# Step sizes of the recurrent mixer: high and low weights in one stationary operand, two passes of products in place of three

## The reference

```python
proj = h @ w_in                                    # h: 256 x 1024
z, xbc, dt, hq, hf, hi, hg = split_cols(proj, ...) # dt: 256 x 8 (SSM_HEADS = 8)
...
dt = jax.nn.softplus(dt.astype(F32) + dt_bias.astype(F32))
a_head = -jnp.exp(a_log.astype(F32))
y = ssd_chunked(xs, dt, a_head, b_in, c_in)        # uses dt, and cumsum(dt * a_head)
```

## Time and profile before

| | |
|---|---|
| device time, three runs | 950.36, 950.37, 950.72 us, median 950.37 us |
| span of the profiled execution | 948.0 us |
| around the span | the median is 2.37 us more than the span; the profiled execution's own device time is not listed |
| PE busy | 934.2 us, 99% |
| DVE busy | 682.3 us, 72% |
| ACT busy | 517.9 us, 55% |
| POOL busy | 92.4 us, 10% |
| mean granted TensorE clock | 0.998 of full speed |

### The profile page before, as it was taken

One profiled execution on the slowest core, in us unless ns is written; L12 is line 12 of the kernel. 1 busy time (PEld: TensorE's weight loads), 2 busy tenths in 40 slices (PEclk: granted clock), 3 DMA queues, 4 the chain that ended last, 5 costly groups with the idle time before them and its releaser, 6 DMA issues.

```text
span 948.0 us, 12990 instructions
## 1 busy us (share of the span) xinstructions
PE 934.2 (99%) x5253; PEld 813.3 (86%) x5253; DVE 682.3 (72%) x880; ACT 517.9 (55%) x711; POOL 92.4 (10%) x111
## 2 busy tenths in 40 slices
PE   8999999999999999999999999999999999999997
PEld 7998888888888898888888888889998888888885
DVE  5899857666657977866776666558999767666663
ACT  5887545444446656965544434468685545334432
POOL 2550200000011100100000000000233010000000
PEclk9999999999999999999999999999999999999999
DMA  9933666565545455146656565556423457656531
GB/s 288 338 129 125 196 230 212 191 204 190 205 141 200 126 175 177 45 134 222 222 181 198 180 197 178 177 157 215 141 90 111 134 158 248 216 179 196 183 109 44
DMA packets 106955, 166.94 MB, mean 176 GB/s; under 512 B 2896, under 2 KB 82848, under 8 KB 106768
## 3 DMA queue, kind: packets, MB, share of 16 engines
q1 hardware_dynamic: 104688, 158.23, 51.1%
q0 software_dynamic: 2208, 7.89, 2.4%
HBM read 165.06 MB, written 1.05 MB: 175 GB/s over the span
## 4 chain that ended last, share of the span: by engine, by line
PE 86%; DVE 7%; ACT 3%; DMA 3%; issue 1%; POOL 0%; ACTq 0%; DVEq 0%; POOLq 0%
PE ps L400 83%; PE ps L408 3%; DMA raw<-in_w_in 2%; DVE wl L1956 2%; DVE SC L2080 1%; ACT wh L1337 1%; DVE fs L2090 1%; ACT SC L1671 1%; ACT junk L1325 0%; DMA h<-in_x 0%; ACT SC L1743 0%; DVE xhl L2017 0%; DVE wl L2118 0%; DVE wl L1970 0%; DVE hs L1999 0%
## 5 line engine op out<-in xcount | busy, mean ns | idle before, releaser
L1956 DVE TENSOR_TENSOR wl<-raw,wh 128x2048 fp32r<-128x2048 f32 (+2 forms) x141 | 318.0, 2259 | 142.3 <-ACT wh L1337 142.2
L1337 ACT ACTIVATE wh<-raw 128x2048 fp32r<-128x2048 f32 (+2 forms) x150 | 281.9, 1886 | 155.3 <-PE ps L400 137.3
L400 PE MATMUL ps<-xhl,wh 128*128 128x512 f32 (+1 forms) x1248 | 254.6, 350 | 0.3 <-ACT wh L1406 0.3
L400 PEld LDWEIGHTS ps<-xhl,wh 128*128 128x128 f32 x1248 | 199.2, 190 | 26.9 <-issue 0.7
L400 PE MATMUL ps<-wh,xhl 128*128 128x512 f32 (+3 forms) x800 | 190.3, 379 | 0.0
L400 PEld LDWEIGHTS ps<-wh,xhl 128*128 128x128 f32 x800 | 142.5, 188 | 24.8
L400 PEld LDWEIGHTS ps<-xhl,wl 128*128 128x128 f32 x1008 | 135.6, 191 | 7.5
L400 PE MATMUL ps<-xhl,wl 128*128 128x256 f32 x1008 | 140.6, 282 | 0.0
L400 PE MATMUL ps<-wl,xhl 128*128 128x512 f32 (+3 forms) x403 | 102.1, 375 | 0.2 <-DVE wl L1970 0.2
L400 PE MATMUL ps<-wh,fh 128*128 128x512 f32 x304 | 91.0, 392 | 0.3 <-DVE fl L2320 0.3
L400 PE MATMUL ps<-wh,fl 128*128 128x512 f32 x304 | 90.2, 390 | 0.0
(11 more groups left out here) (297 smaller groups left out, 833.9 us busy)
## 6 DMA issues: line engine op xcount, KB each, us to landing
raw<-in_ffn_gate SPq DMA_DIRECT2D x22, 1024.0 KB, 5.4
raw<-in_ffn_up SPq DMA_DIRECT2D x22, 1024.0 KB, 5.4
raw<-in_ffn_down SPq DMA_DIRECT2D x22, 1024.0 KB, 4.9
raw<-in_w_up SPq DMA_DIRECT2D x16, 1024.0 KB, 5.4
raw<-in_w_down SPq DMA_DIRECT2D x16, 1024.0 KB, 5.1
raw<-in_s_w_in SPq DMA_DIRECT2D x14, 1024.0 KB, 5.3
raw<-in_w_in SPq DMA_DIRECT2D x9, 1024.0 KB, 9.8
raw<-in_a_w_in SPq DMA_DIRECT2D x6, 1024.0 KB, 5.3
```

What stands on the lines that cost most here:

```text
L400: return e.matmul(o, a, b, start=start, stop=stop, skip_group_check=True)
L1337: e.activation(high_of(i), raw_of(i), ACT.Copy).then_inc(*up("act_high", i))
L1956: e.tensor_tensor(low_of(i), raw_of(i), high_of(i).bitcast(F32), ALU.subtract).then_inc(*up("dve_lo", i))
```

## The change

The high and low parts of the step weights stand side by side in one tile `wdt_hl` (columns 0 to 63 and 64 to 127). In the window of tile k the high columns still feed PSUM rows 0 to 7, and the low columns feed PSUM rows 64 to 71 of the same matmul. Two passes, with `xh` and with `xl`, give both groups of rows: 16 matmuls in place of 24. The product low x low, which was left out before, is now in the sum. The rows 64 to 71 are then added: ACT copies them from PSUM to `dr` row 1, and DVE adds rows 0 to 7, the bias and `dr` row 1 in one instruction. DVE makes the low part of the step weights earlier, right after `norm_low(5, 1)`. POOL zeroes 56 columns of one tile in place of 120 columns of two.

```diff
-        wdt_h, wdt_l = (sb(n, [128, 184], F32R) for n in ("wdt_h", "wdt_l"))
+        wdt_hl = sb("wdt_hl", [128, 184], F32R)
@@ tensor: recurrent()
-                for n, (w, x) in enumerate(((wdt_h, xh), (wdt_h, xl), (wdt_l, xh))):
-                    if n != 1:
-                        e.wait_ge(*(at("dve_dt_low") if n else at("act_dt_high")))
+                e.wait_ge(*at("dve_dt_low"))
+                for x in (xh, xl):
                     for k in range(8):
 
-                        d = mm(ps[0][:, 0:256], w[:, 8 * k:8 * k + 128], x[:, k, :], n == 0 and k == 0, n == 2 and k == 7)
+                        d = mm(ps[0][:, 0:256], wdt_hl[:, 8 * k:8 * k + 128], x[:, k, :], x is xh and k == 0, x is xl and k == 7)
                 d.then_inc(*up("pe_dt"))
@@ scalar: recurrent()
-                e.activation(wdt_h[:, 0:64], wdt, ACT.Copy).then_inc(*up("act_dt_high"))
+                e.activation(wdt_hl[:, 0:64], wdt, ACT.Copy).then_inc(*up("act_dt_high"))
@@
                 e.activation(st[R, 61:62], P("alog")[R], ACT.Exp).then_inc(*up("act_rate"))
+                e.wait_ge(*at("pe_dt"))
+                e.activation(dr[R, 1, :], ps[0][64:72, 0:256], ACT.Copy).then_inc(*up("act_dt_part"))
                 softplus("dt", *(dr[R, i, :] for i in range(4)), junk[R, 0:256])
@@ vector: recurrent()
                 norm_low(5, 1)
+                e.wait_ge(*at("act_dt_high"))
+                e.tensor_tensor(wdt_hl[:, 64:128], wdt, wdt_hl[:, 0:64].bitcast(F32), ALU.subtract).then_inc(*up("dve_dt_low"))
                 lows(S["hi"][0] + 4)
-                e.wait_ge(*at("act_dt_high"))
-                e.tensor_tensor(wdt_l[:, 0:64], wdt, wdt_h[:, 0:64].bitcast(F32), ALU.subtract).then_inc(*up("dve_dt_low"))
                 R = slice(0, 8)
-                e.wait_ge(*at("pe_dt"))
-                e.tensor_scalar(dr[R, 0, :], ps[0][R, 0:256], P("dtb")[R], None, ALU.add).then_inc(
+                e.wait_ge(*at("act_dt_part"))
+                e.scalar_tensor_tensor(dr[R, 0, :], ps[0][R, 0:256], P("dtb")[R], dr[R, 1, :], ALU.add, ALU.add).then_inc(
                     *up("dve_softplus", "dt", "x"))
                 lows(S["hi"][1] + 4)
@@ gpsimd
-            e.memset(wdt_h[:, 64:184].bitcast(F32), 0.0)
-            e.memset(wdt_l[:, 64:184].bitcast(F32), 0.0).then_inc(*up("pool_zero_dt_pad"))
+            e.memset(wdt_hl[:, 128:184].bitcast(F32), 0.0).then_inc(*up("pool_zero_dt_pad"))
```

More of the change, by code:

```diff
@@ L48 @@
                       "act_exp act_map_turned act_latent_out act_back"),
-    "act_recurrent": ("act_bound act_xs act_score act_seg_rows act_dt_high act_hq act_forget act_keys act_log_forget act_rate act_z act_hi act_decay act_between "
+    "act_recurrent": ("act_bound act_xs act_score act_seg_rows act_dt_high act_dt_part act_hq act_forget act_keys act_log_forget act_rate act_z act_hi act_decay act_between "
                       "act_xbc act_hg act_xb act_xs act_cb act_seg act_gated_square act_silu"),
```

## The result

| | median us | range | executions |
|---|---|---|---|
| before | 950.32 | 949.51 to 951.16 | 18 |
| changed | 951.63 | 950.48 to 952.58 | 18 |

The ratio is 1.0015, 95% interval 1.0009 to 1.0022: the change makes the kernel slower by 1.3 us, 0.9 to 2.1. The forecast was 951.5, within 0.2% of the time before.

The account below looks back on a forecast made before the run. PE, busy 99% of the span, was taken as the bound. Products -1.10, wait at xbc3 +1.98, rest of the wait at `score(8)` +0.28 give +1.16 us: span 949.2, time 951.5 us; 8 in 10 for 950.2 to 952.8.

Parts of the forecast that it names:

- PE's saving: At the step sizes: eight fewer matmuls and no wait for the low part start hf0 1.10 us earlier.
- The hand-over: After the step-size products: DVE waits for ACT's copy, then adds it; DVE 1.35 us late at mend, bounds 1.05 to 1.65.
- xbc3: PE's first meeting with late DVE: waits some 1.9 us for the turned step sizes, gain becomes a 0.88 us loss.
- `score(8)`: PE's second meeting: ACT, hanging on DVE, has 0.19 us in hand at queries(1); start 1.16 us late, lasting to the end.
- the likeliest case: Whole kernel: a loss of about 1.2 us, inside the 1.9 us a measurement can tell; chance 0.72.
- The 2.37 us between span and time: Whole kernel: median of runs lies 2.37 us above the profiled span; same distance added to the forecast span of 949.2.
- The clock rival: At the wait before xbc3: PE's clock falls to 1.2 GHz, adding 2.6 us, 954.1 us in all; chance 0.08.
- The absorption rival: DVE between 652 and 674 us: slack absorbs the delay, the 1.10 us saving stands, 949.3 us; between 949.3 and 950.9: 0.14.

Follow-up runs that it names:

- hand-over alone: Kernel before, still three passes and 24 matmuls, plus only ACT's copy of PSUM rows 64 to 71 and DVE's adding of it; 951.16 us, ratio 1.0011.
- turned first: Changed kernel with DVE's copies of the turned step sizes out of bank 0 moved ahead of conv(0); 951.10 us, ratio 1.0010.
- the longer wait: Changed kernel with DVE's copies of the turned step sizes moved behind the low part of hq0; 954.38 us, ratio 1.0047.
- both ends: Changed kernel with ACT's copy and alog exp earlier, xbc1's low part later, turned step sizes copied before conv(0), decays earlier; 948.54 us, ratio 0.9984.

## Why the prediction was right

**PE's saving**: forecast 1.10 us at hf0, found 1.12. The low part of the step weights is made at 630.2, long before.

**The hand-over**: the copy took 0.38 us (0.42 forecast), the sum 0.47 (0.47), Abs waited 0.54 behind the copy. The low part of xbc1 stood between the sum and `1+u`, as forecast, and Ln waited 0.24 us for `1+u`. `mend` came 1.42 us late, against 1.35. The load of xbc1 has a part in that: it lands when it does, and ACT starts the chain behind it. In the profiles ACT's table load at the head of the chain starts 3.49 us after the step sizes before, 3.64 and 3.63 in the two of the changed kernel, 3.41 in the hand-over alone and 3.47 in turned first. DVE was late by 1.42, 1.41, 1.19 and 1.26 there. Taken from that start the hand-over cost 1.26 to 1.28 us in all four, 0.08 under my sum, and the landing added up to 0.15.

**xbc3**: a PE wait of 1.9 us was forecast, 1.87 found (by the starts 1.98 forecast and 2.03 found, 30.90 to 32.93 us after the step sizes); PE 0.88 late there, 0.91 found.

**`score(8)`**: forecast 1.16 us late; 1.25 in the execution in which the clock stayed, and ACT's wait for PE was gone as forecast. From there to the end both kernels take 252.77 us, so the shift stays. This is the likeliest case as it was written, within 0.1 us at each step. That the median of runs (951.63) lies 0.13 from the forecast is partly luck: it stands between the two groups, 950.8 and 952.3. The forecast was for the group in which the clock stays up, and that one lost 0.85 and 0.62 us by its times, not 1.16; executions with the lower clock, which the forecast had left to a rival, brought the median up to it. The 2.37 us between span and time in the forecast did no harm, because adding them to both kernels is the same as adding 1.16 to the time before, but it is no constant: the executions of the changed kernel lie 1.8 us above their spans.

**The clock rival** was given 0.08 and 2.6 us on top. That the clock would leave 1.00 behind the wait was one of the signs that the prediction had named for being wrong, and in the profiled execution it came. It happened, in 12 of 29 executions by their mean clock, and where it was profiled it cost 1.24 us at `score(8)` (2.49 against 1.25 late). Two things were off. The chance: the end of the program, with a fall some 2.3 us after the last matmul, and the first microseconds, with none after 1.18, left 1.9 us open, and I treated a gap between two bounds as if it were nearly safe. The fall itself came 0.7 us after PE had resumed, so that a wait shorter than such a bound was no protection. The price: I took a group of 24 wholly at half pace, 2.9 us; the measured group took 1.59 more, since its matmuls started before the fall and ended after the rise, and 0.35 of it was hidden behind ACT. Even the 24 of the longer wait, all at 0.50, took 2.4 more and not 2.9.

**The absorption rival** is refuted: DVE's 0.5 us of small gaps took up none of the delay. DVE was 1.42 late at `mend` and 1.42 at the turned copy.

## What to carry to other kernels

On an engine that is busy 99% of the time a removed instruction is worth its time only if, at each place where that engine waits next, the other engines have as much slack as is saved: here they had 0.6 us at the first and 0.2 at the second, and the hand-over took more than that from them. Read the slack at the next meetings before pricing the saving; and place a hand-over by what is queued in front of it, since a copy of 0.4 us made DVE 1.3 us late behind other work and 0.4 ahead of it, and only the first reached PE. A new wait of PE of some 2 us is also a risk to its clock, with a price of its own: in this kernel 12 of 29 executions had the lower mean clock.

## What the runs showed of the hardware

- The granted clock fell to 1.2 GHz behind a PE wait of 1.87 us in one profiled execution, some 0.7 us after PE had resumed, and stayed at full speed behind the same 1.87 us in another; behind 3.90 us it was at 0.50 before PE resumed. In the kernels whose waits before xbc3 and `score(8)` are 0.53 us or less (hand-over alone and both ends, among others) no mean clock is below 0.998.
- At 1.2 GHz matmuls of 256 columns start some 0.22 us apart (24 in 5.29 us, all at 0.50) in place of 0.12 (24 in 2.88 us): 1.84 times, not twice.
- The page "TensorE: Matmul & The Clock Gate" of the Trainium skill, section "HAM oscillation", says that gaps in PE's work bring its clock down. One profile of the changed kernel agrees, with the fall behind 1.87 us; the other shows the same gap without a fall.
- An ACT copy of 8x256 from PSUM partitions 64 to 71 to SBUF partitions 0 to 7 takes 0.38 us and needed no table load between an Exp and an Abs.
